# Three transformer blocks on one core: the compressed branch placed between the parts of the last projection, stick-breaking in three passes, two output products by halves

## The reference, cut to what matters

```python
def stick_breaking_attention(q, k, v):            # 8 heads of 64, per query block of 128
        z = jnp.einsum('bhqd,bhkd->bhqk', q_blk, k) * scale
        past = k_idx[None, :] < t_idx[:, None]
        log_stay = jnp.where(past, jax.nn.log_sigmoid(-z), 0.0)
        between = lax.cumsum(log_stay, axis=3, reverse=True) - log_stay
        w = jnp.where(past, jnp.exp(jax.nn.log_sigmoid(z) + between), 0.0)
        return jnp.einsum('bhqk,bhkd->bhqd', w, v)

def fox_mixer(h, w_in, b_f, w_out):               # layer 6 of the kernel
    ...
    return (o * jax.nn.silu(z)) @ w_out

def nsa_mixer(h, w_in, pe_k, w_ck1, w_ck2, pe_v, w_cv1, w_cv2, w_out):   # layer 7
    proj = h @ w_in                               # 1024 -> 3632 columns
    q, kc_raw, vc_raw, ks_raw, vs_raw, kw_raw, vw_raw, gate_raw, z = jnp.split(proj, ...)
    # compressed branch: 15 blocks of 32 tokens, stride 16, 4 groups of keys
    kc = compress_blocks(kc_raw, pe_k, w_ck1, w_ck2)   # silu((blk + pe) @ w1) @ w2
    vc = compress_blocks(vc_raw, pe_v, w_cv1, w_cv2)   # w1: 2048 x 256, w2: 256 x 64
    kc = rope_partial(kc, cmp_end)
    lg_c = jnp.einsum('bsgrd,bcgd->bgrsc', q, kc) * scale
    p_c = softmax(where(mask_c, lg_c, NEG));  p_c = where(mask_c, p_c, 0.0)
    o_c = jnp.einsum('bgrsc,bcgd->bsgrd', p_c, vc)
    ... # with 256 tokens every block is selected: o_s and o_w are causal attentions
    o = g[..., 0:1] * o_c + g[..., 1:2] * o_s + g[..., 2:3] * o_w
    return (o.reshape(B, S, W) * jax.nn.silu(z)) @ w_out
```

## Time and profile before

| | |
|---|---|
| time, median of 3 runs | 2174.99 us (2173.08 to 2178.22) |
| the profiled execution | 2174.94 us, its span 2173.2 us |
| mean granted TensorE clock | 0.969 of full |
| TensorE busy | 2027.1 us, 93% (9737 products) |
| VectorE, ScalarE busy | 1543.9 us (71%), 1313.3 us (60%) |
| GpSimd busy | 81.7 us (4%) |
| chain that ended last, by engine | TensorE 83%, VectorE 8%, ScalarE 5%, issue 2%, DMA 1% |
| split of a full chunk | 1.91 us on ScalarE (line 963), 2.28 us on VectorE (line 967) |
| copy of 128 x 512 out of a bank by ScalarE | 0.67 us (line 445) |
| first work of VectorE in the last attention | at 2076.2 us |

### The profile page before, as it was taken

One profiled execution on the slowest core, in us unless ns is written; L12 is line 12 of the kernel. 1 busy time (PEld: TensorE's weight loads), 2 busy tenths in 40 slices (PEclk: granted clock), 3 DMA queues, 4 the chain that ended last, 5 costly groups with the idle time before them and its releaser, 6 DMA issues.

```text
span 2173.2 us, 26349 instructions
## 1 busy us (share of the span) xinstructions
PE 2027.1 (93%) x9737; PEld 1669.7 (77%) x9737; DVE 1543.9 (71%) x1725; ACT 1313.3 (60%) x1401; POOL 81.7 (4%) x93
## 2 busy tenths in 40 slices
PE   5999986899999999999999999999999999998687
PEld 3886775688877778888888888888887878787576
DVE  5547772644457688988898988989897844665565
ACT  6445547444445567878777777878786754454243
POOL 0000200000000041000000000000001001000000
PEclk9999999999999999999999999999999999999698
DMA  9655551455544279999999999999999956154100
GB/s 332 207 175 175 176 190 53 145 180 188 185 163 155 78 276 393 366 382 362 389 362 384 370 380 384 371 380 368 383 370 373 353 169 208 60 161 134 39 1 29
DMA packets 185103, 535.16 MB, mean 246 GB/s; under 512 B 12465, under 2 KB 23749, under 8 KB 185030
## 3 DMA queue, kind: packets, MB, share of 16 engines
q1 hardware_dynamic: 174624, 516.85, 65.1%
q10 hardware_dynamic: 8582, 11.02, 1.5%
q0 software_dynamic: 1824, 6.31, 1.1%
HBM read 521.02 MB, written 13.12 MB: 246 GB/s over the span
## 4 chain that ended last, share of the span: by engine, by line
PE 83%; DVE 8%; ACT 5%; issue 2%; DMA 1%; DVEq 0%; ACTq 0%; POOLq 0%; POOL 0%; SPq 0%
PE bank L408 24%; PE bank L410 23%; PE bank L409 23%; DVE WL L967 3%; PE bank L523 2%; ACT WH L963 2%; PE bank L535 1%; PE bank L2378 1%; PE bank L314 1%; DMA ring<-in_od_we_up 1%; PE bank L549 1%; PE bank L547 1%; PE bank L545 1%; PE bank L375 1%; PE bank L2147 1%
## 5 line engine op out<-in xcount | busy, mean ns | idle before, releaser
L967 DVE TENSOR_TENSOR WL<-ring,WH 128x2048 fp32r<-128x2048 f32 (+1 forms) x487 | 1100.8, 2280 | 350.7 <-ACT WH L963 347.3
L963 ACT ACTIVATE WH<-ring 128x2048 fp32r<-128x2048 f32 (+1 forms) x487 | 925.8, 1912 | 423.0 <-PE bank L410 397.8
L408 PE MATMUL bank<-WH,XTH 128*128 128x512 f32 (+2 forms) x1936 | 760.4, 393 | 30.6 <-DVE WL L967 11.9
L409 PE MATMUL bank<-WL,XTH 128*128 128x512 f32 (+2 forms) x1936 | 751.2, 388 | 0.0
L410 PE MATMUL bank<-WH,XTL 128*128 128x512 f32 (+2 forms) x1936 | 750.8, 388 | 0.0
L408 PEld LDWEIGHTS bank<-WH,XTH 128*128 128x128 f32 x1936 | 370.7, 191 | 116.2 <-issue 23.8
L410 PEld LDWEIGHTS bank<-WH,XTL 128*128 128x128 f32 x1936 | 370.1, 191 | 74.1
L409 PEld LDWEIGHTS bank<-WL,XTH 128*128 128x128 f32 x1936 | 370.4, 191 | 70.2
L408 PE MATMUL bank<-WH,HTH 128*128 128x512 f32 x540 | 211.6, 392 | 3.9 <-DVE HTL L2064 2.0
L410 PE MATMUL bank<-WH,HTL 128*128 128x512 f32 x540 | 209.9, 389 | 0.0
L409 PE MATMUL bank<-WL,HTH 128*128 128x512 f32 x540 | 209.7, 388 | 0.0
(11 more groups left out here) (409 smaller groups left out, 1477.7 us busy)
## 6 DMA issues: line engine op xcount, KB each, us to landing
ring<-in_od_we_gate SPq DMA_DIRECT2D x112, 1024.0 KB, 7.1
ring<-in_od_we_up SPq DMA_DIRECT2D x112, 1024.0 KB, 8.7
ring<-in_od_we_down SPq DMA_DIRECT2D x112, 1024.0 KB, 8.2
ring<-in_w_in SPq DMA_DIRECT2D x20, 1024.0 KB, 5.2
ring<-in_fox_w_in SPq DMA_DIRECT2D x16, 1024.0 KB, 5.3
ring<-in_nsa_w_in SPq DMA_DIRECT2D x14, 1024.0 KB, 5.0
ring<-in_w_ada SPq DMA_DIRECT2D x12, 1024.0 KB, 8.5
ring<-in_ev_w_in SPq DMA_DIRECT2D x12, 1024.0 KB, 6.4
```

The lines of the kernel that those rows point to most:

```text
L408: nc.tensor.matmul(out, x[0], wt[0][:, k, :], start=start, stop=False, skip_group_check=check)
L409: nc.tensor.matmul(out, x[0], wt[1][:, k, :], start=False, stop=False, skip_group_check=check)
L963: nc.scalar.activation(wh, slot_ap(n, nk, width), ACT.Copy).then_inc(hi_made, 1)
L967: nc.vector.tensor_tensor(wl, slot_ap(n, nk, width), wh.bitcast(F32), ALU.subtract).then_inc(lo_made, 1)
```

## The change

It does five things. (1) In projection 2, TS2 and TD2 are done ahead of and inside job 5 (`heads2`, `heads2_rotated`; a new argument `during` gives ScalarE and VectorE work between splits and copies, and TensorE's `beside` can also be keyed by job and chunk). (2) Stick-breaking runs in three passes over all 8 heads: Abs and Exp; Ln; the last Exp. Each head has its own bank (`ST_BANK`) and its own tile (`ST_E`); the mask is added to the scores at once, the second scoring and VectorE's two maskings go. (3) The whole compressed branch of layer 7 lies between the chunks of P7, and so do the head transposes of the queries; the order of P7's columns and of the chunks in the stream changes; blocks lie in KT and in P, the hidden layer in O; the second layer is done in full-precision products (8 instead of 12), the scores in 16 products of 64 columns instead of 32 of 32; the block tiles are zeroed by GpSimd during layer 6's end. (4) In layers 6 and 7 the first half of O's columns is gated inside the attention (at head 13 of 16, at unit 29 of 32), and transposes and product run in two halves. (5) `mask_causal` shares a tile with `mask_past` and is made later; the router's weights RW lie in `scr` and are loaded later. The diff, cut to its core:

```diff
@@ streams
-        in5_order = [0, 512, 1536, 2048, 1024]
+        in5_order = [1024, 0, 512, 1536, 2048]
+        c_in5 = [cols(w["nsa_w_in_3"], c, 512) for c in in5_order[:3]]
+        c_in5.append([])
+        for j in range(2):
+            first_layer("nsa_w_ck1_3", j)
+            c_in5[3].append(half_cols(in5_order[3], j))
+        c_in5.append([half_cols(in5_order[4], 0)])
+        first_layer("nsa_w_cv1_3", 0)
+        c_in5[4].append(half_cols(in5_order[4], 1))
+        c_ck2.append(cols(w["nsa_w_ck2_3"], 0, DH)[0][0])
+        first_layer("nsa_w_cv1_3", 1)
...
+        c_z5 = [[half_cols(2608, 0)]]
+        c_ck2.append(cols(w["nsa_w_cv2_3"], 0, DH)[0][0])
+        c_z5[0].append(half_cols(2608, 1))
@@ ends of layers
+        def gate_half(dve, signal, half_):
+            o = O[:, :, half_ * 512:half_ * 512 + 512]
+            nc.vector.tensor_tensor(o, o, P[:, :, 3072 + half_ * 512:3584 + half_ * 512], ALU.mult).then_inc(signal, 1)
+            if i == 13:
+                dve.wait_ge(grouped, A6.g + 1)
+                gate_half(dve, g6, 0)
...
+            if i == 29:
+                dve.wait_ge(w_added, 6)
+                gate_half(dve, g7, 0)
@@ GpSimd
+            pool.wait_ge(g6, 2)
+            nc.gpsimd.memset(FLAT(KT), 0.0).then_inc(ones_set, 1)
+            nc.gpsimd.memset(P[:, :, 3072:4096], 0.0).then_inc(ones_set, 1)
+            nc.gpsimd.memset(scr[:, 1152:1664], 0.0).then_inc(ones_set, 1)
@@ ScalarE
-            P2.act(act, {1: tables, 2: lambda: roots(act, stat[:, 16:48])})
-            TS2.act(act)
-            TD2.act(act)
+            P2.act(act, {1: tables, 2: lambda: roots(act, stat[:, 16:48]), 4: lambda: TS2.act(act)},
+                   {5: lambda: TD2.act(act)})
             for i in range(9):
                 if i < 8:
                     act.wait_ge(st_z, i + 1)
-                    ...
+                    st_write(("abs", i), nc.scalar.activation(ST_E[i], ST_BANK[i][:, 0:384], ACT.Abs))
                 if i >= 1:
-                    ...
+                    act.wait_ge(act_chain, written["abs", i - 1])
+                    st_write(("exp", i - 1), nc.scalar.activation(ST_E[i - 1], ST_E[i - 1], ACT.Exp, scale=-1.0))
+            for i in range(8):
+                act.wait_ge(act_chain, written["exp", i])
+                nc.scalar.activation(ST_E[i], ST_E[i], ACT.Ln, bias=1.0).then_inc(st_ln, 1)
+            for i in range(8):
+                act.wait_ge(st_r, i + 1)
+                nc.scalar.activation(ST_E[i], ST_BANK[i][:, 0:384], ACT.Exp).then_inc(st_w, 1)
@@ ScalarE, layer 7
+            P7.act(act, {1: lambda: block_hi(0, 0), 2: lambda: block_hi(0, 1),
+                         3: lambda: (TQ7.act(act, 0, 4), block_hi(1, 0)), 4: lambda: hidden_act(1),
+                         5: lambda: hidden_copy(1)},
+                   {3: lambda: hidden_act(0), 4: lambda: (hidden_copy(0), block_hi(1, 1)), 6: weights_exp})
+            TQ7.act(act, 4)
@@ VectorE, layer 7
+            P7.dve(dve, {0: doubled, 1: key_blocks, 2: value_blocks, 3: turned_queries, 4: compressed_keys,
+                         5: compressed_turned}, {4: lambda: block_lo(1, 1), 6: compressed_weights, 7: weights_turned})
+            TQ7.dve(dve, 4)
@@ TensorE
+            P2.pe(pe, T2, {5: heads2, (5, 1): heads2_rotated})
+            for i in range(8):
+                z = ST_BANK[i]
+                nc.tensor.matmul(z[:, 0:384], identb[:, :], mask_past[:, :], start=True, stop=False, skip_group_check=True)
+                nc.tensor.matmul(z[:, 0:256], k[:, 128:256], q, start=False, stop=True, skip_group_check=True)
+                nc.tensor.matmul(z[:, 256:384], k[:, 0:128], q[:, 128:256], start=False, stop=True,
+                                 skip_group_check=True).then_inc(st_z, 1)
+            for i in range(11):
+                if i < 8:
+                    pe.wait_ge(st_sp, i + 1)
+                    ... # three products with neg_tri and neg_ones into the same bank
+                if i >= 3:
+                    j = i - 3
+                    pe.wait_ge(st_w, max(j + 1, 2))
+                    ... # the three products with the values
@@ TensorE, layer 6 (layer 7 alike)
             pe.wait_ge(g6, 1)
-            TO6.pe(pe)
-            OUT6.pe(pe, operand=TO6, closes=True)
+            TO6[0].pe(pe)
+            A6.wait(pe)
+            OUT6[0].pe(pe, last_=False, operand=TO6[0])
+            pe.wait_ge(g6, 2)
+            TO6[1].pe(pe)
+            OUT6[1].pe(pe, first=False, operand=TO6[1], closes=True)
@@ TensorE, layer 7
+            P7.pe(pe, T7, {2: raw_blocks, 3: lambda: first_layer_part(0, 0), (3, 1): lambda: first_layer_part(0, 1),
+                           4: turn_queries, (4, 1): lambda: (turn_hidden(0), first_layer_part(1, 0)),
+                           5: lambda: (second_layer(0), first_layer_part(1, 1)),
+                           6: lambda: (turn_hidden(1), turn_compressed()),
+                           (6, 1): lambda: (compressed_scores(), second_layer(1)), (7, 1): turn_weights})
+            pe.wait_ge(roped7, 3)
+            pe.wait_ge(q_Tc, 2)
+            TQ7.pe(pe, 4)
+            ... # per half of the tokens: four products with the compressed values
+            P7.wait(pe)
+            TQ7.wait(pe)
```

More of the change, by code:

```diff
@@ L427, in pe @@
                         pe.wait_ge(proj_act, self.ba + c - 1)
-                    for n, k0, nk in chunks:
+                    for part, (n, k0, nk) in enumerate(chunks):
+                        if (c, part) in beside:
+                            beside[c, part]()
                         wt = take(pe, n)
@@ L1486, in _ @@
             roots(act, stat[:, 8:16])
+            with nc.allow_non_contiguous_dma(reason="eight columns"):
+                act.dma_start(RW[:, :, :], t["od_router_2"][0].rearrange("(k p) e -> p k e", p=128)).then_inc(rw_in, 16)
             OUT2[0].splits(act)
@@ L1578, in _ @@
             A6.act(act)
-            TO6.act(act)
-            OUT6.splits(act)
+            for i in range(2):
+                TO6[i].act(act)
+                OUT6[i].splits(act)
             norm_act(act, 5, T7)
@@ L1606, in _ @@
             act.dma_start(GAIN, t["final_g_3"].partition_broadcast(128)).then_inc(gfin2_in, 16)
-            TO7.act(act)
-            OUT7.splits(act)
+            for i in range(2):
+                TO7[i].act(act)
+                OUT7[i].splits(act)
             for tt in range(TT):
@@ L2461, in _ @@
-            for i in range(2):
-                if i == 0:
-                    TQ7.wait(pe)
-                pe.wait_ge(c_lo, i + 1)
-                for n, k0, nk in c_ck[i][0]:
-                    wt = take(pe, n)
-                    for k in range(nk):
-                        last = three(bank[4 + i][:, 0:256], [x[:, k0 + k, :] for x in xblocks], wt, k, k0 + k == 0,
-                                     k0 + k == 15, check=True)
-                    last.then_inc(consumed, 1)
+            TO6[0].pe(pe)
@@ new lines, in first_layer_part, with turn_hidden @@
+            def first_layer_part(i, j):
+                pe.wait_ge(c_lo, 2 * i + j + 1)
+                if i:
+                    pe.wait_ge(turn_dve, TQ7.bd + 1)
+                wt = take(pe, c_ck1[2 * i + j])
+                for k in range(8):
+                    last = three(bank[4 + i][:, 0:256], [XBH[:, k, :], XBL[:, k, :]], wt, k, j == 0 and k == 0,
+                                 j == 1 and k == 7, check=True)
+                last.then_inc(consumed, 1)
+            def turn_hidden(i):
@@ L2474, in _, with second_layer @@
                 last.then_inc(c_hT, 1)
[L2475 to L2476 removed]
+            def second_layer(i):
+                pe.wait_ge(c_hTh, i + 1)
+                wt = take(pe, c_ck2[i])
                 for k in range(2):
[L2478 removed]
+                    for part in wt:
+                        last = nc.tensor.matmul(bank[6 + i][:, 256:256 + DH], CHT[i][:, k * 128:k * 128 + 128],
+                                                part[:, k, :].bitcast(F32), start=k == 0 and part is wt[0],
+                                                stop=k == 1 and part is wt[1], skip_group_check=True)
@@ new lines, in compressed_scores @@
+            def compressed_scores():
+                pe.wait_ge(c_kTc, 1)
+                pe.wait_ge(c_s, 2)
+                TQ7.wait_queries(pe)
+                for tt in range(TT):
+                    out = bank[4 + tt][:, :].rearrange("p (q r g c) -> p r g q c", q=2, r=2, g=4)
+                    for g in range(4):
+                        for r in range(2):
+                            last = nc.tensor.matmul(out[:, r, g], QT[:, 2 * g + r, tt * 128:tt * 128 + 128], KCT[:, g, :, :],
+                                                    start=True, stop=True, skip_group_check=True)
+                    last.then_inc(q_s, 1)
```

441 lines of the change are left out of this document (216 added, 225 removed).

## The result

The changed kernel took 2114.53 us, median of four runs (2113.34 to 2116.79); the kernel before 2176.6 beside it (2173.08 to 2179.19). The ratio is 0.9717, 95% interval 0.9699 to 0.9735: faster by 62 us, for 64 forecast (2111 us, range 2098 to 2127). The profiled execution took 2113.54 us, its span 2111.8, at a mean clock of 0.977. TensorE is busy 2008.6 us (95% of the span), VectorE 1534.0, ScalarE 1294.8.

The account below looks back on a forecast made before the run. TensorE, busy 93% of the span, was taken as the bound, with time to be had only where it idles or runs slow. Gains 20.9 + 39.7 + 1.3 + 2.5 = 64.4 us gave 2110.5, say 2111 us; range 2098 to 2127.

Parts of the forecast that it names:

- stick-breaking: Stretch from projection 2 to the next attention's first score: three table loads, score at 355.3 instead of 376.3, gain 20.9 us.
- layer 6's end: Gating and output product by halves: 4.6 earlier, less 1.0 inside the attention and 2.3 at the seam, gain 1.3 us.
- projection and branch: Last projection with compressed branch inside: 83.1 + 22.1 + 7.3 stalls + 1.7 clock = 114.2, then 7.1; gain 39.7 us.
- layer 7's end: Output product by halves: 5.8 earlier, less 1.0 inside the attention and 2.3 at the seam, gain 2.5 us.
- Rival (d): Drain of 1.38 us at each table switch ends stick-breaking 4.1 us later, total 2115; chance 0.02.
- rival (e): TensorE stays at half clock to the end of stick-breaking, total 2119; chance 0.05.
- The bound for no half clock: Upper bound of stick-breaking's gain if TensorE never runs at half speed there: 22.7 us.
- one more: In the last projection, one further clock loss of 1.7 us, at the scores and the wait ahead of the weights.
- Rival (a): Steps' waits come along into the last projection: half of 24.7 us stays, 2123, all of it 2135; chance 0.18.
- Rival (b): All fits in the last projection and the clock holds: no 7.3, no 3.4 us, total 2100; chance 0.12.
- Rival (c): TensorE's clock falls at a step in each job of the last projection, never rises: +76 us, 2187; chance 0.03.
- attention units over 1.7 us: Sign of a wrong forecast: an attention whose units take over 1.7 us each.

Follow-up runs that it names:

- the second experiment: Changed kernel with each head's Ln put right behind its Exp in stick-breaking's first pass, 14 more table switches: 2133.42 us, ratio 0.9811.
- the head-by-head kernel: Changed kernel with stick-breaking's old loop over heads, a table load before each Exp and Ln, head transposes left moved: 2128.55 us, ratio 0.9785.
- the kernel with whole gates: Changed kernel with gates, transposes and output products of layers 6 and 7 in one piece again, behind the attention: 2116.14 us, ratio 0.9732.
- the kernel with the gate chunk earlier: Changed kernel with a Silu and the window keys' rope moved behind the splits the gate product waits for: 2109.32 us, ratio 0.9681.
- after: The changed kernel itself, against the kernel before: 2114.53 us, ratio 0.9717; run again 2113.5 us, ratio 0.9708.
- the gain's kernel: Changed kernel with ScalarE's load of the final gain moved behind the first half's split in layer 7's end: 2110.08 us, ratio 0.9699.
- all three: Changed kernel with gate chunk split earlier, compressed maxima ahead of the split and final gain loaded later: 2102.57 us, ratio 0.9659; again 2101.52 us, 0.9655.

## Why the prediction was right, and where it was off

| step | forecast gain | measured |
|---|---|---|
| stick-breaking | 20.9 | 21.05 (376.25 to 355.20) |
| between them, up to layer 6's last reciprocal | 0 | -0.5 |
| layer 6's end | 1.3 | 2.3 |
| projection and branch | 39.7 | 37.8 |
| layer 7's end | 2.5 | 0.8 |
| sum | 64.4 | 61.4 |

The measured column is one pair of profiles, so it adds up to the difference of their spans (2173.2 - 2111.8). The -0.5 lies ahead of layer 6's attention, in stages that differ by more than that between profiles of the same instructions. That the total came so close is in part luck: layer 6 gave 1.0 more than forecast, the projection and layer 7 together 3.6 less.

**Stick-breaking** came out term by term: three loads of 1.283, the first sum at 338.83 for 338.9, three heads' sums at half clock (0.86 from the sum over 256 columns to the next at 340.70, 0.43 at 343.96), the first score at 355.20 for 355.3. Rival (d), the drain, fell with the second experiment; rival (e), half clock to the end, with the row at 343.96, where the full speed comes back as before. The times of the head-by-head kernel show that the passes make the larger part of it. The bound for no half clock was added up wrong: three heads at full speed save 3 x 0.84 = 2.5 us, which makes 23.4 and not 22.7.

**The last projection** took 116.8 us for 114.2. The stalls were 1.2 for 1.2 in job 3, 1.5 for 1.8 at the gate chunk, 3.0 for 4.3 at the weights: 5.6 for 7.3. The two largest were named with their cause, and the two kernels that take these causes away show it: one hole goes, the other shrinks, and the time falls. (By the recorded numbers, TensorE there at 32.1 and turning at 36.9, the last stall would have been 4.8 and not 4.3, which is further off.) The term that was mis-sized is the clock: 3.4 us forecast (1.7 from before and one more), 6.8 found. The step behind it priced the fall at the gate product at what it had been before, though the same step put a hole right in front of that product. With the hole that fall is 5.1, without it 3.4; the fall behind the weights' turns, 1.7, is the "one more" of the text. Why the fall without a hole costs 3.4 here and 1.7 in the kernel before, with the same 48 products, no run separates: here 4 full-precision products of 64 columns and 24 products of 256 stand right ahead of them, there products of 512. The rest is work: TensorE's busy time of 111.18 less the 83.08 of before and the 5.1 us of added clock loss leaves 23.0 for an inserted 22.1, an estimate from these rows. Behind the projection came 6.7 us to the last attention's first work for 7.1.

**Rival (a)**, the waits coming along, would have kept half of 24.7 us; 5.6 us of waits are there, fewer than the forecast had. Moving the scores and the softmax back out shows that they gain 5.6 us inside. (Of the ten rows that make the 32.0 us, eight name VectorE, 29.7 us, and two ScalarE, 2.3; the prediction reads all ten as VectorE.) **Rival (b)** (2100, no stalls and no fall) was too early here, but it names what was to be had: with the one hole gone, the other cut to 0.97 us and the gain's load moved, the kernel took 2101.5, and still has the wait in job 3 and 3.4 us of clock. **Rival (c)** stayed away: behind each fall the large products brought the clock back, as after 1978.61 in the earlier trace rows.

**The ends of the layers.** In layer 6 the product starts 4.7 us earlier behind the last reciprocal (2.5 for 7.2) and the seam costs 2.2, as said. The term that fails is the 1.0 lost inside the attention: the last group takes 12.05 us with the gate for 12.06 without, so the gain is 2.3 and not 1.3. In layer 7 the product starts 5.8 earlier within its stretch, just as said (2141.82 to 2075.77 is 66.05, of which the last reciprocal brought 60.25); the seam costs 2.2 for 2.3, and the attention is 0.4 longer for 1.0. Of that 0.4 the gate has 0.1 at most (last group 12.15 for 12.09); the rest is in the second group (14.49 for 14.13), where the kernel with whole gates has it too. What was left out is the clock: the first half of the product took 13.5 us for 11.0, and 5.8 - 2.2 - 0.4 - 2.5 = 0.7. As other profiles of the same end took 11.0, this miss is the execution's as much as the kernel's. The load that ScalarE issues ahead of the split, with its wait for the attention's last group, held the start for another 1.0 us, as the experiment shows; the prediction counts the issue of the router's weights and not this one.

One of the signs named for a wrong forecast could tell nothing: attention units over 1.7 us. A full group of 8 units in the last attention takes 14.12 us, 1.77 a unit, in both kernels.

## What to carry to other kernels

A hole of 1.5 to 2 us on the engine that bounded cost its length and about as much again where narrow work stood around it (3.4 us for 1.5, 3.8 for 2.0), because the clock fell there for longer or fell at all, in most profiles though not in all: price such a hole twice, and remove it first. When work is moved into another stage, the gain is decided by which split or copy stands in front of the one that the engine waits for; two reorderings on the helper engines gave 7 us, a ninth of what the whole change did. Compare stretches between two marks inside one profile, not spans, when a difference is under half a per cent.

## What the runs showed of the hardware

The granted clock fell while TensorE had no idle time at all. In the kernel with the gate chunk earlier its busy time is 10.00 of 10.00 us in 1966.16 to 1976.16, and in the middle of the run of 48-column products the start to start changes from 0.11 to 0.21 us:

```profile
1972.18 0.27 PE L433 MATMUL bank<-WL,XTH 128*128 128x48 f32 x1
1972.29 0.33 PE L434 MATMUL bank<-WH,XTL 128*128 128x48 f32 x1
1972.45 0.39 PE L432 MATMUL bank<-WH,XTH 128*128 128x48 f32 x1
1972.66 0.39 PE L433 MATMUL bank<-WL,XTH 128*128 128x48 f32 x1
...
1978.69 0.63 PE L433 MATMUL bank<-WL,XTH 128*128 128x512 f32 x1
1979.12 0.43 PE L434 MATMUL bank<-WH,XTL 128*128 128x512 f32 x1
```

Full speed is back at 1979.39. So "busy" in a profile does not say whether the clock will hold; in the kernel with 16 of these products for 48 it held. The Trainium skill, "TensorE: Matmul & The Clock Gate", section "What's actually happening", has it that activity releases the throttle; here it went from 2.4 to 1.2 GHz in the midst of what the profile counts as activity.

What stays open is when it falls behind a wait: the same code had it in one profile and not in the next, both behind the weights' turns (0.83 in after and in the gain's kernel, 1.00 with whole gates) and in the last product (a first half of 11.0 us in one run of all three, 13.9 in the other).
